# A two-block network on one core: RMS norms as factors in the weights' splits and in the results, and the first loads in another order

## The reference

```
def _rmsnorm(x, g):
    var = mean(x * x, axis=-1)
    return x * rsqrt(var + 1e-6) * g

for layer in range(2):
    h = _rmsnorm(x, norm1_g[layer])
    proj = h @ w_in[layer]                      # 1024 x 2588
    o_a = _hgrn2(...)  # gates: f = lb + (1 - lb) * sigmoid(z), chunked linear recurrence
    o_b = _nsa(...)    # compressed, selected and window attention
    o_c = _fox(...)    # attention with forget gates
    x = x + concat(o_a, o_b, o_c) @ w_o[layer]
    h2 = _rmsnorm(x, norm2_g[layer])
    x = x + square(relu(h2 @ w_up[layer])) @ w_down[layer]
```

## Time and profile before

| | |
|---|---|
| runs | 3864.67, 3852.85, 3854.48 us; median 3854.48 |
| profiled execution | 3855.84 us, its span 3854.6 |
| PE busy | 87% of the span, 16600 products and transposes |
| PEld, DVE, ACT, POOL busy | 72%, 59%, 47%, 7% |
| TensorE clock, mean over the span | 0.925 of full |
| DMA | 591 MB, a mean of 153 GB/s |

### The profile page before, as it was taken

How to read it: one execution, slowest core, us unless ns; L and a number is a source line. 1 busy time by engine, 2 the same in 40 slices (tenths; PEclk the granted TensorE clock), 3 DMA queues, 4 the chain that set the end, 5 groups by cost and what they waited for, 6 DMA issues and landing times. The chain is left out here.

```text
span 3854.6 us, 42165 instructions
## 1 busy us (share of the span) xinstructions
PE 3343.2 (87%) x16600; PEld 2765.3 (72%) x16601; DVE 2268.0 (59%) x3531; ACT 1817.6 (47%) x2713; POOL 255.6 (7%) x282
## 2 busy tenths in 40 slices
PE   5988899998989899998678499999859877999993
PEld 4878777776788678777447488888647765888882
DVE  4845343426655342433544499999743646999995
ACT  3323332323223332322533288888632616888883
POOL 0101000001101000000000111111000201111110
PEclk9988999999989899999789699999979978999996
DMA  3120122211110122222001389998723234899893
GB/s 127 47 73 1 66 75 85 103 66 67 46 52 1 66 88 100 84 79 80 1 22 55 143 332 365 363 365 350 288 96 112 67 144 178 350 367 368 356 371 136
DMA packets 133865, 591.16 MB, mean 153 GB/s; under 512 B 29440, under 2 KB 35328, under 8 KB 107936
## 3 DMA queue, kind: packets, MB, share of 16 engines
q1 hardware_dynamic: 113856, 570.13, 38.3%
q0 software_dynamic: 19808, 18.29, 1.4%
HBM read 598.81 MB, written 39.99 MB: 166 GB/s over the span
## 5 line engine op out<-in xcount | busy, mean ns | idle before, releaser
L188 PE MATMUL ps<-r,r 128*128 128x512 f32 (+4 forms) x10880 | 2541.5, 393 | 73.3 <-DVE r L721 32.2
L188 PEld LDWEIGHTS ps<-r,r 128*128 128x128 f32 x10880 | 2021.1, 190 | 533.7 <-issue 77.7
L3141 DVE TENSOR_TENSOR r<-mem,r 128x1024 fp32r<-128x1024 f32 x768 | 908.9, 1222 | 103.0 <-ACT r L3089 94.7
L3089 ACT ACTIVATE r<-mem 128x1024 fp32r<-128x1024 f32 x768 | 792.1, 1062 | 199.0 <-PE ps L188 185.8
L721 DVE TENSOR_TENSOR r<-mem,r 128x512 fp32r<-128x512 f32 (+2 forms) x512 | 342.5, 680 | 745.1 <-ACT r L703 743.3
L703 ACT ACTIVATE r<-mem 128x512 fp32r<-128x512 f32 (+2 forms) x512 | 312.0, 618 | 947.2 <-PE ps L188 946.8
L545 PE MATMUL ps<-mem 128*128 128x128 f32 x384 | 70.3, 353 | 173.7 <-DVE mem L2173 93.9
L545 PEld LDWEIGHTS ps<-mem 128*128 128x128 f32 x384 | 60.8, 186 | 182.9 <-issue 166.1
L188 PE MATMUL ps<-mem 128*128 128x64 f32 (+5 forms) x744 | 140.2, 350 | 34.9 <-DMA mem<-in_nsa_cmp_w 15.0
L188 PEld LDWEIGHTS ps<-mem 128*128 128x128 f32 x744 | 120.9, 239 | 49.1 <-DMA mem<-in_nsa_cmp_w 15.5
L3002 POOL DMA_INDIRECT yd<-mem,memu x64 | 65.5, 1023 | 1009.3 <-ACT mem L3114 993.3
(11 more groups left out here) (332 smaller groups left out, 2867.9 us busy)
## 6 DMA issues: line engine op xcount, KB each, us to landing
mem<-in_w_up SPq DMA_DIRECT2D x80, 2048.0 KB, 17.7
mem<-in_w_down SPq DMA_DIRECT2D x80, 2048.0 KB, 8.1
mem<-in_w_gate SPq DMA_DIRECT2D x64, 2048.0 KB, 12.7
mem<-in_w_in SPq DMA_DIRECT2D x10, 2048.0 KB, 8.1
mem<-in_odd_w_qkv SPq DMA_DIRECT2D x6, 2048.0 KB, 10.5
mem<-in_w_o SPq DMA_DIRECT2D x4, 2048.0 KB, 13.9
mem<-yd SPq DMA_DIRECT2D x8, 1024.0 KB, 8.7
mem<-in_rel SPq DMA_DIRECT2D x16, 512.0 KB, 3.5
```

Of the source, the lines that this page charges most:

```text
L188: r = e.matmul(out, a, b, start=start and i == 0, stop=stop and i == n - 1, skip_group_check=skip)
L3089: act.e.activation(wh, w, ACT.Copy).then_inc(*self.S["ex_wh"](self.l, e, i))
L3141: dve.e.tensor_tensor(wl, w, wh.bitcast(F32), SUB).then_inc(*self.S["ex_wl"](self.l, e, i))
```

## The change

1. **Setup.** The identity (64 KB of the constants) and the first layer's gain are loaded ahead of X, and counted with it. The first chunk of w_in is issued right behind X, the other constants behind that, and the second chunk of w_in last. PE, ACT and DVE wait for X, the identity and that gain alone. The rest of the constants is awaited where it is used: by POOL at the mixer's start, by DVE at the gates' bound, and by PE ahead of the mixer's fourth piece.
2. **Turns.** All turns of X are turns of raw rows. norm1_1 stands behind ffn_0 as even_x stands behind ffn_1; they stay stages of their own (an option to weave a turn into the product ahead of it is in the code, and isn't used: `turn` is None in every stage). The turn ahead of `Out` writes to other memory.
3. **Gain.** `high` and `low` multiply a piece of w_in or w_up by the gain of its rows.
4. **Factor in the mixer.** The squares go beside pieces 0 to 3 on ACT; mean, root and reciprocal beside piece 4; there the bound of the gates is made too, in layer 0. For the gates, whose results have tokens along the columns, DVE writes the four factors' diagonals and PE spreads them over the partitions by four products with ones, behind piece 6; ACT copies that row, and DVE multiplies the four results. The other results are multiplied in their evictions.
5. **Factor in Ffn.** The squares go beside pieces 0 to 3; mean and reciprocal on DVE beside piece 4; the adds to X multiply by it. Hidden blocks lie at other places in memory.

```diff
+        o, w = OFF["ident"]
+        early = [(self.ident, A["c_main"][:, o:o + w])]
+        pairs = [(self.m(co + w, NCONST - w), A["c_main"][:, w:NCONST])]
...
-            pairs.append((g["g1"], A["norm1_g"][l]))
+            (pairs if l else early).append((g["g1"], A["norm1_g"][l]))
...
+        for o, i in K.early_loads:
+            sp.e.dma_start(o, i).then_inc(*S["d_x"]("x"))
         for t in range(4):
             sp.e.dma_start(K.X[:, t, :], K.A["x"][0, 128 * t:128 * t + 128, :]).then_inc(*S["d_x"]("x"))
+        K.load_weights(-1, most=1)
         for o, i in K.first_loads:
             sp.e.dma_start(o, i).then_inc(*S["d_c"]("c"))
         K.load_weights(-1)
 
     def pe(self, pe):
-        pe.wait_ge("d_c", "c")
-
-    def pool(self, pool):
-        pool.wait_ge("d_c", "c")
+        pe.wait_ge("d_x", "x")
 
     def act(self, act):
-        K = self.K
-        act.wait_ge("d_c", "c")
         act.wait_ge("d_x", "x")
-        w = K.lbw[:, 0:4]
-        act.wait_ge("lb_v", "sub")
-        act.e.activation(w, w, ACT.Exp).then_inc(*self.S["lb_a"]("exp"))
 
     def dve(self, dve):
...
+def bound_dve(K, dve):
+
+    S, v = K.S, dve.e
+    w = K.lbw[:, 0:4].rearrange("p (j l) -> p j l", j=2)
+    mx = K.lbw[:, 4:6]
+    dve.wait_ge("d_c", "c")
+    dve.then("lb_v", v.tensor_reduce(mx, K.lg, AX.X, MAX))
+    v.tensor_tensor(w, K.lg, bc(mx, 2, 2), SUB).then_inc(*S["lb_v"]("sub"))
+    dve.wait_ge("lb_a", "exp")
+    dve.then("lb_v", v.tensor_reduce(mx, w, AX.X, ADD))
+    dve.then("lb_v", v.reciprocal(mx, mx))
+    dve.then("lb_v", v.tensor_tensor(w, w, bc(mx, 2, 2), MUL))
+    v.tensor_tensor(K.lb[:, 0, :], w[:, :, 0], w[:, :, 0], SUB).then_inc(*S["lb_v"]("l0"))
+    dve.then("lb_v", v.tensor_tensor(K.lb[:, 1, :], w[:, :, 0], w[:, :, 1], ADD))
+    dve.then("lb_v", v.tensor_tensor(K.lb[:, 1, :], K.lb[:, 1, :], w[:, :, 0], SUB))
+    dve.then("lb_v", v.tensor_scalar(K.olb, K.lb, -1.0, 1.0, MUL, ADD))
...
+    def pe_unit(self, pe, u):
+        t, half = divmod(u, 2)
+        src = self.src(t)
+        if self.ready:
+            pe.wait_ge(*self.ready(t))
+        if u >= 4:
+            pe.wait_ge("nx_lo", self.name, u - 4)
+        for k in range(4):
+            c = 128 * (4 * half + k)
+            r = pe.e.transpose(self.ps(u)[:, k, :], src[:, c:c + 128], self.K.ident)
+        r.then_inc(*self.S["nx_turn"](self.name, u))
+
+    def act_unit(self, act, u):
+        act.wait_ge("nx_turn", self.name, u)
+        act.e.activation(self.place(self.hr, u), self.ps(u), ACT.Copy).then_inc(*self.S["nx_hi"](self.name, u))
+
+    def dve_unit(self, dve, u):
+        K = self.K
+        if self.lo is None:
+            t, half = divmod(u, 2)
+            dve.wait_ge("nx_turn", self.name, u)
+            r = dve.e.tensor_copy(K.HT[:, 4 * half:4 * half + 4, 128 * t:128 * t + 128], self.ps(u))
+        else:
+            dve.wait_ge("nx_hi", self.name, u)
+            r = dve.e.tensor_tensor(self.place(self.lr, u), self.ps(u), self.place(self.hr, u).bitcast(F32), SUB)
+        r.then_inc(*self.S["nx_lo"](self.name, u))
...
+        scale = 1.0 if job.gain is None else job.gain[:, kk:kk + 1]
+        act.e.activation(wh, w, ACT.Copy, scale=scale).then_inc(*self.S["dn_hi"](self.p0 + i))
...
     def low(self, dve, i):
+        job, kk = self.plan[i]
         w, wh, wl = self.piece(i)
         dve.wait_ge("dn_hi", self.p0 + i)
-        dve.e.tensor_tensor(wl, w, wh.bitcast(F32), SUB).then_inc(*self.S["dn_lo"](self.p0 + i))
+        if job.gain is None:
+            r = dve.e.tensor_tensor(wl, w, wh.bitcast(F32), SUB)
+        else:
+            r = dve.e.scalar_tensor_tensor(wl, w, job.gain[:, kk:kk + 1], wh.bitcast(F32), MUL, SUB)
+        r.then_inc(*self.S["dn_lo"](self.p0 + i))
...
+        if factor is not None:
+            r = dve.e.scalar_tensor_tensor(x, ps, factor[:, j:j + 1], x, MUL, ADD)
...
+def squares(K, act, name, i, junk):
+
+    act.e.activation(junk, K.X[:, i, :], ACT.Square, accum_out=K.rms[:, i:i + 1]).then_inc(*K.S["nx_sq"](name, i))
...
-                r = act.e.activation(dst(j), view(ps[:, c:c + n]), ACT.Copy)
+                r = act.e.activation(dst(j), view(ps[:, c:c + n]), ACT.Copy, scale=K.rms[:, j:j + 1])
...
-                r = dve.e.tensor_copy(dst(j), view(ps[:, c:c + n]))
+                r = dve.e.tensor_scalar(dst(j), view(ps[:, c:c + n]), K.rms[:, j:j + 1], None, MUL)
...
+            if i == 3:
+                pe.wait_ge("d_c", "c")
...
+            if i == 6:
+                self.pe_factors(pe)
...
+    def root_act(self, act, i):
+
+        K, S, sid = self.K, self.S, self.name
+        if i < 4:
+            squares(K, act, sid, i, K.m(self.F.PQo + 1024 * i, 1024))
+        elif i == 4:
+            act.wait_ge("nx_norm", sid, "mean")
+            act.e.activation(K.rms, K.rms, ACT.Sqrt).then_inc(*S["nx_sq"](sid, "root"))
+            if self.F.l == 0:
+                bound_act(K, act)
+        elif i == 6:
+            act.wait_ge("nx_turn", sid, "row")
+            act.e.activation(self.F.WS[0], K.bank[7][:, :], ACT.Copy).then_inc(*S["nx_hi"](sid, "row"))
+
+    def root_dve(self, dve, i):
+        K, S, sid, v = self.K, self.S, self.name, dve.e
+        if i == 4:
+            dve.wait_ge("nx_sq", sid, 3)
+            v.tensor_scalar(K.rms, K.rms, 1.0 / D, 1e-6, MUL, ADD).then_inc(*S["nx_norm"](sid, "mean"))
+            dve.wait_ge("nx_sq", sid, "root")
+            dve.then("nx_norm", v.reciprocal(K.rms, K.rms))
+            for t in range(4):
+                r = v.tensor_scalar(self.F.WS[1][:, 128 * t:128 * t + 128], K.ident, K.rms[:, t:t + 1], None, MUL)
+            r.then_inc(*S["nx_norm"](sid, "diagonal"))
+            if self.F.l == 0:
+                bound_dve(K, dve)
+
+    def pe_factors(self, pe):
+        K, S, sid = self.K, self.S, self.name
+        pe.wait_ge("nx_norm", sid, "diagonal")
+        for t in range(4):
+            c = slice(128 * t, 128 * t + 128)
+            r = pe.e.matmul(K.bank[7][:, c], K.ones, self.F.WS[1][:, c], start=True, stop=True)
+        r.then_inc(*S["nx_turn"](sid, "row"))
+
     def gates_a(self, act, st, job, j, ps):
         F, S = self.F, self.S
         if j < 2:
-            act.e.activation(F.Qf[:, j, :], ps, ACT.Copy, scale=0.125).then_inc(*S["dn_ev_a"](self.name, 0, j))
             return
-        act.e.activation(F.Kf[:, j - 2, :], ps, ACT.Exp, scale=-1.0).then_inc(*S["dn_ev_a"](self.name, 0, j))
+        act.wait_ge("dn_ev_v", self.name, 0, j)
+        act.e.activation(F.Kf[:, j - 2, :], F.KT[1][:, j - 2, :], ACT.Exp,
+                         scale=-1.0).then_inc(*S["dn_ev_a"](self.name, "gate", j))
+
+    def gates_v(self, dve, st, job, j, ps):
+        F, S, v = self.F, self.S, dve.e
+        dve.wait_ge("nx_hi", self.name, "row")
+        if j < 2:
+            r = v.scalar_tensor_tensor(F.Qf[:, j, :], ps, 0.125, F.WS[0], MUL, MUL)
+        else:
+            r = v.tensor_tensor(F.KT[1][:, j - 2, :], ps, F.WS[0], MUL)
+        r.then_inc(*S["dn_ev_v"](self.name, 0, j))
...
+    def act_beside(self, act, i):
+        if i < 4:
+            squares(self.K, act, self.name, i, self.K.m(self.K.L0 + 1024 * i, 1024))
+
+    def dve_beside(self, dve, i):
+
+        K, v = self.K, dve.e
+        if i == 4:
+            dve.wait_ge("nx_sq", self.name, 3)
+            dve.then("nx_norm", v.tensor_scalar(K.rms, K.rms, 1.0 / D, 1e-6, MUL, ADD))
+            dve.then("nx_norm", v.reciprocal(K.rms, K.rms))
...
+    F, M = [First(K, l) for l in range(2)], Even(K)
     add(Setup, "setup")
+    add(Turn, "norm1_0", F[0].MIXo, lambda t: K.X[:, t, :])
     for l in range(2):
-        F = First(K, l)
-        add(Turn, f"norm1_{l}", F.MIXo, gain=K.g[l]["g1"], scratch=F.W)
-        M = add(Mixer, f"mixer_{l}", F)
-        add(Causal, f"causal_{l}", F, M)
-        add(Turn, f"mix_{l}", base, src=lambda t, F=F: F.MIX[:, t, :])
-        add(Out, f"out_{l}", ("o", l), base)
+        mixer = add(Mixer, f"mixer_{l}", F[l])
+        add(Causal, f"causal_{l}", F[l], mixer)
+        add(Turn, f"mix_{l}", base, lambda t, l=l: F[l].MIX[:, t, :], base + 4096)
         hlo = base + 16384
-        add(Turn, f"norm2_{l}", hlo, gain=K.g[l]["g2"], scratch=base + 8192)
-        add(Ffn, f"ffn_{l}", l, hlo)
+        add(Out, f"out_{l}", ("o", l), base + 4096, base)
+        add(Turn, f"norm2_{l}", hlo, lambda t: K.X[:, t, :])
+        add(Ffn, f"ffn_{l}", l, hlo, None)
+        add(Turn, ("norm1_1", "even_x")[l], (F[1].MIXo, M.lo)[l], lambda t: K.X[:, t, :])
     for l in range(2):
```

297 lines of the change are left out of this document (122 added, 175 removed).

## The result

The changed kernel takes 3806.81 us (median of 4 runs, 3799.32 to 3811.54) beside 3859.57 of the kernel before (4 runs, 3852.85 to 3868.01): ratio 0.986, interval 0.9831 to 0.9889. It is faster, by less than forecast: 3785 was said, and 3777 to 3801 as the range. A later timing on one chip gave 3808.02 (5 runs) beside 3867.53 (9 runs), 0.984 (0.9827 to 0.9854).

The account below looks back on a forecast made before the run. PE is busiest, so its standstills ahead of the norm turns and at the start were taken as the bound: 3855.8 - 45.5 (three turns) - 28.2 (start) + 3.0 (mixers) = 3785.1, forecast 3785 us, range 3777 to 3801.

Parts of the forecast that it names:

- the 1.0 charged behind the first product: Start: PE's wait for the constants at the mixer's fourth piece, charged at 1.0 us.
- The base: Whole kernel: the profiled execution's 3855.84 us, from which the gains were subtracted and the mixers' cost added.
- The clock term: Three turns inside the program: first pieces behind them run at full clock, 6.5 of the 45.5 us gained.
- rival A: New turns: the clock stays at the lower level, price 6.5 us, time 3792; chance 0.14.
- the plain turn: Raw rows turned ahead of the even layer's projection: 9.78 us from first add to first product, taken for the new turns.
- The start: Start to first product: X in at 10.3 us, first product at 17.5 instead of 46.65; gain 28.2 us.
- B: Start: first weights in only at 23 us, first product at 24.9, 6.4 us more, time 3792; chance 0.08.
- The mixers: Both mixers: four products and four multiplications for the gates' factor cost 1.5 us each, 3.0 together.
- The splits behind DVE's wait: Mixers: splits of pieces 11 on, queued behind DVE's wait for the factor row, due 8 us later: hidden.
- C: Mixers: PE stands at its four products until squares and root are done, 6.0 us each, time 3797; chance 0.06.
- D: Weight splits: the scaled splits become the bound of the 240 pieces, slower, 3886 at 3.2 us per piece; chance 0.01.
- E: Turns: the change moves the norm's chain and doesn't shorten it, time 3856; chance 0.01.

Follow-up runs that it names:

- The fill: The changed kernel with products of no use put into PE's pauses ahead of the causal stages and behind their first turns: 3804.91 us, ratio to before 0.984.
- the old loads: The changed kernel with the loads at the start in the order of before, all engines waiting for all constants: 3828.33 us.

## Why the prediction was wrong in size

The sum, term by term, against the means of four profiles of each kernel (span 3861.9 before, 3805.3 after), each row the difference of a stretch in the timelines (the 28.2 holds the 1.0 charged behind the first product):

| stretch | said | measured |
|---|---|---|
| start to first product | -28.2 | -27.7 |
| mixer_0 | +1.5 | +1.4 |
| out_0 and norm2_0 | -13.3 | -12.1 |
| ffn_0 and norm1_1 | -2.4 - 12.5 | -12.8 |
| mixer_1 | -1.6 + 1.5 | +1.7 |
| out_1 and norm2_1 | -13.3 | -12.7 |
| ffn_1 | -2.4 | -1.2 |
| causal_0 and causal_1 | 0 | +6.4 + 0.4 |
| all else | 0 | -0.1 |
| sum | -70.7 | -56.6 |

**The base failed first.** "The median of the runs is 1.4 below that execution and inside their spread, so I leave it": of the 34 executions of before that were timed in the end, with the profiled one, the median is 3865.9, and only two are faster than it. Its profile had both causal stages near the shortest seen, 174.70 and 175.02. The four profiles of before average 3863.2, 7.3 above the base. The rest is the 14.1 us by which the sum fell short: 3785.1 + 7.3 + 14.1 = 3806.5, beside a mean of 3806.6. The executions come from several chips, and no run separates a chip's share.

**The clock term failed.** "Of it 6.5 through the clock": of the 14.1, 7.0 are missing in the five stretches of the three turns. Between the first add and the end of the first piece the three turns gave 41.6 us in the mean for the 45.5 said. Of these 3.9, 0.5 is the add with the factor ahead of mixer_1, charged at nothing: 13.38 in the execution with full clock there, beside 12.83. The other 3.4 are the clock. 0.6 are mixer_1's own, behind its first piece (below), and the rest lies in the products between, 1.7 of it in out_0 and out_1.

The norm2 turns kept full clock in seven of eight cases (9.78 or 9.79 us from add to product, once 10.57), but their first pieces took 3.04 to 3.07 us in four cases and 4.25 to 4.32 in four, 5.49 in none. The turn ahead of mixer_1 fell in three of four executions: 7.8 to 8.9 us from first transpose to first product instead of 7.15, and first pieces of 4.6. So rival A holds there, with PE 3.1 to 3.2 us without work ahead of it, and at more than its price: A kept 9.78 us for the turn, which took 10.9 to 12.0. The sample that spoke against A, the plain turn of the earlier trace rows, came from one kernel: it had 7.09 us in three executions of before and 8.91 in the fourth, and in all four of the changed kernel 7.8 to 8.7 (ahead of it the add with the factor now takes 2.73). Over all eight profiles with raw turns that aren't woven, the turns with PE 2.7 us without work ahead of them kept full clock in 15 of 16, and those with 3.1 to 3.2 lost it in 13 of 16. No run changes that pause alone, so it goes with the fall and isn't shown to cause it. Out_0 ran partly at the lower clock in two of the four executions, out_1 in one.

The Trainium skill (TensorE: Matmul & The Clock Gate, "PE-mode transpose") says that the full clock doesn't engage for transposes, which don't count as PE-busy in the same way; by that every turn would end at the lower clock. The window of 454.90 to 464.70 with 1.00 speaks against "every". The turn ahead of mixer_1 goes with it, but no run tells whether it was the transposes or the pause ahead of them. The turn at the start speaks against the page: with nothing but transposes behind it, PE goes from one each 0.21 us (10.3 to 13.3) to one each 0.11 (16.0 to 16.9). The window of the earlier trace rows at 0.50 has nine in 1.93 us, and sixteen took 1.94 at 1.00.

**"Nothing" elsewhere failed.** I had taken the stages that the change doesn't touch as unchanged. Causal_0 cost 6.4 us more in the mean; both causal stages make 6.8 of the 14.1. That the clock does it is shown (the same instructions at 0.82 and 0.89, in one kernel); that the change brings it on is likely by ten executions and not shown, and by what stays open. The fill shows that PE's pause at the stage's start alone isn't it.

**The start held**, by errors that cancel: the turn took 8.9 to 9.3 us instead of 7.09, X landed up to 1.1 earlier than 10.3, and the 1.0 charged for the constants wasn't due. In the turn, 1.28 us are the table load. The transposes also began at the lower clock's pace, which the sum had at full clock: sixteen in 3.68 us, and 3.38 with the old loads, where X had long been in. PEclk reads 1.00 there all the same, so the pace is what shows it. (10.3 + 7.09 is 17.4, where the prediction has 17.5.) B didn't come: the first weights were in when ACT came to them. The reading of the DMA rows by order of issue was right on both arrivals.

**The mixers held in layer 0**, 1.6 for 1.5 at level 0. The 1.4 of the whole stage is partly luck: three executions give 0.5 to 0.9, the fourth 3.4. The price of the four products had a wrong source: line 1665 of the earlier trace rows is the causal stage's turn, twelve transposes at the lower clock; 0.93 was said and 1.05 came. Layer 1 cost 2.9 at level 0 and 2.1 over what lies behind its first piece: my sum of the path, 5.6 us from the end of piece 6 to the gates' first instruction, fits layer 0 (46.09 - 40.42 = 5.67), where the bound's exponential has brought the table shortly before; in layer 1 ACT's table load stands in that path, and it is 876.80 - 869.86 = 6.94. The splits behind DVE's wait were "hidden"; there, PE waits 0.89 us for one. C didn't come: the row was copied without a wait of PE for the squares.

**D and E are out**: the splits' 0.72 and 0.75 us stand under 2.78 per piece, and leaving the gain out changed no feed-forward stage.

**The range failed by the same neglect.** It held each rival alone, but not the scatter of the executions: 3799.32 to 3815.92 for the changed kernel, eleven of them, and 3852.85 to 3875.55 for the one before. A range around a kernel of this program has to hold some 8 to 11 us to either side for that alone. It didn't hold C together with A or B either: by their prices these are 3804 (3785.1 + 12.0 + 6.5), not "near 3799". The direction, faster, was right.

## What to carry to other kernels

Before a profiled execution is taken as the base of a sum, see where it stands among the runs and whether its stages have had a lucky clock; a term that hangs on the clock needs more than one sample of the row it is read from. Chains that stand alone between two stretches of products are worth their full length, and the timeline gives it to some tenths; weaving the turn into the products ahead gives part of it once more, and the clock stayed at 1.00 in three of the four turns woven here. When work moves onto a new path, look for the table load that it brings with it.
